# A vector of the adaptive layer norm moved from the sparse attention to the third FFN

## What is computed

```python
c_act = jax.nn.silu(c)
for i in range(DEPTH):                                   # DEPTH = 2
    mod = c_act @ ada_w[i] + ada_b[i]                    # 1024 -> 9 * 1024
    sh1, sc1, gt1, sh2, sc2, gt2, sh3, sc3, gt3 = jnp.split(mod, N_MOD, axis=-1)
    h = h + 0.5 * gt1 * swiglu(modulate(h, sh1, sc1), ffn_w_gu[i, 0], ffn_w_down[i, 0])
    u = modulate(h, sh2, sc2)
    m = dsa_mixer(u, ...) if i % 2 == 0 else rwkv7_mixer(u, ...)
    h = h + gt2 * m
    h = h + 0.5 * gt3 * swiglu(modulate(h, sh3, sc3), ffn_w_gu[i, 1], ffn_w_down[i, 1])
```

## Time and profile before

| | us |
|---|---|
| median of 3 runs | 1331.88 (1331.15 to 1332.82) |
| the profiled execution, in all | 1335.42 |
| its span in the profile | 1333.7 |
| TensorE busy | 1195.2 (90%), mean granted clock 0.911 |
| VectorE busy | 947.3 (71%) |
| ScalarE busy | 551.1 (41%) |
| the 256 multiply-adds of L1720 | 168.4 + 24.0 |

### The profile page before, as it was taken

The page is one execution under the profiler, slowest core; times in us unless marked ns, Lnnn a source line. Parts: engine busy times, 40 slices in busy tenths (PEclk is TensorE's granted clock), DMA queues, the critical chain, the costliest instruction groups (busy, mean ns, idle before and its releaser), DMA issues.

```text
span 1333.7 us, 20285 instructions
## 1 busy us (share of the span) xinstructions
PE 1195.2 (90%) x7950; PEld 943.0 (71%) x7950; DVE 947.3 (71%) x1291; ACT 551.1 (41%) x789; POOL 9.6 (1%) x27
## 2 busy tenths in 40 slices
PE   5799999877598899999899999798897968999998
PEld 1588887756256678887678888566676856788886
DVE  5888886876644788887788886698785495644443
ACT  2544444534233444444544444447341232444331
POOL 1000000000000000000000000000000000000000
PEclk9999999889557989999999999888896688999999
DMA  9789986563002678888578888421623020755540
GB/s 330 254 300 315 314 301 212 172 234 100 1 0 64 217 268 299 297 297 285 167 254 304 299 307 234 149 59 69 198 77 98 4 98 1 252 189 189 185 162 32
DMA packets 185852, 252.88 MB, mean 190 GB/s; under 512 B 30449, under 2 KB 121585, under 8 KB 185777
## 3 DMA queue, kind: packets, MB, share of 16 engines
q1 hardware_dynamic: 181554, 251.32, 56.2%
q10 hardware_dynamic: 4224, 0.52, 0.3%
HBM read 249.71 MB, written 2.10 MB: 189 GB/s over the span
## 4 chain that ended last, share of the span: by engine, by line
PE 75%; DVE 14%; DMA 4%; issue 3%; ACT 3%; SPq 1%; POOL 0%; DVEq 0%; ACTq 0%; POOLq 0%
PE bank L695 20%; PE bank L697 20%; PE bank L696 20%; DVE ada_acc L1720 2%; DVE gu_lo L1792 2%; PE bank L894 2%; DMA front<-in_ada_w_dram 1%; PE bank L755 1%; PE bank L1135 1%; PE bank L904 1%; PE bank L921 1%; PE bank L1020 1%; DVE dn_lo L1802 1%; ACT gu_hi L1269 1%; SPq L530 1%
## 5 line engine op out<-in xcount | busy, mean ns | idle before, releaser
L695 PE MATMUL bank<-gu_hi,xT_hi 128*128 128x512 f32 (+1 forms) x944 | 377.8, 400 | 34.0 <-DVE gu_lo L1792 9.1
L696 PE MATMUL bank<-gu_lo,xT_hi 128*128 128x512 f32 (+1 forms) x944 | 374.1, 396 | 0.0
L697 PE MATMUL bank<-gu_hi,xT_lo 128*128 128x512 f32 (+1 forms) x944 | 374.1, 396 | 0.0
L1792 DVE TENSOR_TENSOR gu_lo<-raw,gu_hi 128x2048 fp32r<-128x2048 f32 (+1 forms) x108 | 239.3, 2252 | 11.8 <-ACT gu_hi L1269 11.7
L695 PEld LDWEIGHTS bank<-gu_hi,xT_hi 128*128 128x128 f32 x944 | 182.6, 193 | 78.5 <-issue 16.0
L696 PEld LDWEIGHTS bank<-gu_lo,xT_hi 128*128 128x128 f32 x944 | 182.4, 193 | 39.1 <-issue 0.7
L697 PEld LDWEIGHTS bank<-gu_hi,xT_lo 128*128 128x128 f32 x944 | 181.9, 193 | 38.3
L1269 ACT CAST gu_hi<-raw 128x2048 fp32r<-128x2048 f32 (+1 forms) x108 | 199.7, 1881 | 18.4 <-DMA raw<-in_dsa_w_in_dram 8.0
L1720 DVE SCALAR_TENSOR_TENSOR ada_acc<-ada_raw,cact,ada_acc 128x512 f32<-128x512 f32 x224 | 168.4, 752 | 12.3 <-DMA ada_raw<-in_ada_w_dram 1.3
L695 PE MATMUL bank<-dn_hi,hT_hi 128*128 128x512 f32 x320 | 136.6, 427 | 6.6 <-DVE dn_lo L1802 6.6
L1802 DVE TENSOR_TENSOR dn_lo<-raw,dn_hi 128x2048 fp32r<-128x2048 f32 x40 | 91.7, 2291 | 68.2 <-ACT dn_hi L1280 68.2
(11 more groups left out here) (283 smaller groups left out, 1245.2 us busy)
## 6 DMA issues: line engine op xcount, KB each, us to landing
raw<-in_ffn_w_gu_dram SPq DMA_DIRECT2D x176, 512.0 KB, 8.9
ada_raw<-in_ada_w_dram SPq DMA_DIRECT2D x128, 512.0 KB, 6.7
raw<-in_ffn_w_down_dram SPq DMA_DIRECT2D x40, 1024.0 KB, 5.1
raw<-in_rwkv_w_rkv_dram SPq DMA_DIRECT2D x24, 512.0 KB, 5.0
raw<-in_dsa_w_in_dram SPq DMA_DIRECT2D x16, 512.0 KB, 5.1
front<-in_ada_w_dram SPq DMA_DIRECT2D x8, 512.0 KB, 7.8
last_raw<-in_ffn_w_down_dram SPq DMA_DIRECT2D x4, 1024.0 KB, 6.1
raw<-in_dsa_w_out_dram SPq DMA_DIRECT2D x8, 512.0 KB, 5.7
```

Source lines behind the costliest of these rows:

```text
L695: nc.tensor.matmul(out_ap, sta_hi, mov_hi, start=start, stop=False, skip_group_check=True)
L696: nc.tensor.matmul(out_ap, sta_hi, mov_lo, start=False, stop=False, skip_group_check=True)
L697: return nc.tensor.matmul(out_ap, sta_lo, mov_hi, start=False, stop=stop, skip_group_check=True)
L1792: nc.vector.tensor_tensor(gu_lo[:, par, ks, 0:width], buf[:, i, 0:4 * width].rearrange("p (k c) -> p k c", k=4), gu_hi[:, par, ks, 0:width ...
```

## The change

The attention builds two vectors, 14 and 15. Vector 16 is built in the first block of FFN 1, which has 16 to 25 now, and FFN 2 has 26 to 35, ten instead of nine. The waits on `mods_ready` follow the new numbers. `slice_of`, which maps a vector to its layer and column, is unchanged: in FFN 1 the first two belong to layer 0. With ten vectors, FFN 2 takes the branches that FFN 0 and FFN 1 take for the total of the tenth (`if nv == NB - 1`).

```diff
-    ADA_FFN = ((4, 10), (17, 10), (27, 9), (36, 0))
+    ADA_FFN = ((4, 10), (16, 10), (26, 10), (36, 0))
     ADA_DSA = 14
@@ sync, dsa
-                    if i in (1, 2, 3):
+                    if i in (1, 2):
                         load_ada(ADA_DSA - 1 + i, 0, ADA_DSA - 1 + i)
@@ tensor, dsa
-                    if i in (1, 2, 3):
+                    if i in (1, 2):
                         ada_total(ADA_DSA - 1 + i, TB[i % 2])
...
-                        pe.wait_ge(mods_ready, ADA_DSA + 3)
+                        pe.wait_ge(mods_ready, ADA_DSA + 2)
@@ vector, ffn
-                dve.wait_ge(mods_ready, (14, 27, 36, 36)[f])
+                dve.wait_ge(mods_ready, (14, 26, 36, 36)[f])
@@ vector, dsa
                 for i in range(3):
                     rest_in(i + 1)
-                    ada_products(ADA_DSA + i)
+                    if i < 2:
+                        ada_products(ADA_DSA + i)
```

## The result

The changed kernel took 1339.39 us in the median of 5 runs (1338.1 to 1344.95), the kernel before 1331.88 (1330.22 to 1335.25): a ratio of 1.006, 95% interval 1.0033 to 1.0086. Slower, and by more than forecast: +7.5 us where I had +4.0. (The ratios in this document are not the quotients of the medians beside them; the two can differ by 0.1%.)

The account below looks back on a forecast made before the run. TensorE carries three quarters of the chain, but its waits in the attention's projection and at the third FFN's end count. 10.4 - 6.4 = +4.0 us on the median 1331.88 gives 1335.9, range 1331.9 to 1339.6.

Parts of the forecast that it names:

- Attention, which wait goes: Attention's input projection: without vector 16's products the norm starts 7.3 us earlier, block 14 at 284.0, stall 1.1 us, not 8.4.
- What is late next: Attention: block 15 waits for its load, the q norm and the z copy; starts at 297.1 after a 2.1 us stall.
- Clock: Attention: block 14 stays at full clock; after the stall before block 15 the clock falls, a loss of 1.7 us.
- Attention, the size: Attention: block 15 begins 8.1 us earlier, less 1.7 us of clock, gain 6.4 us; bounds 2.6 to 8.8.
- Second FFN, nil: Second FFN: still builds ten vectors, 16 to 25, with equally large transfers covered by TensorE work; cost nil.
- Third FFN: Third FFN's end: later last down block delays RWKV's first weights' cast 10.1 us; with 0.3 of clock, cost 10.4 us.
- The sum: Whole kernel: third FFN's 10.4 less attention's 6.4 gives +4.0 us; 1339.4 on the profiled execution, 1335.9 as forecast median.
- The first (small loads not held): Third FFN's end: small loads are not held, delay 6.2 + 0.3, sum +0.1, 1332.0 us; chance 0.14.
- the second (the clock stays up): Attention's block 15: clock stays up as after the 1.56 us stall, sum +2.3, 1334.2 us; chance 0.12.
- the third (the attention keeps only 2.6 us): Attention: block 15's load lands late, gain 2.6, sum +7.8, 1339.7 us; chance 0.11.
- The fourth (the late cast is covered): Third FFN's end: k weights' cast waits without holding the silu; with cover for all -6.4, 1325.5 us; chance 0.07.

Follow-up runs that it names:

- this part alone: Kernel before with only the third FFN changed: it builds ten vectors, the last one made a second time as the tenth; 1344.14 us, ratio 1.0076.
- the silu's place: Changed kernel, at the third FFN's end the silu and hidden casts of the last block's first half come before rounding RWKV's first weights; 1335.95 us, ratio 1.0.
- before with small loads early: Kernel before with the ten small loads of the RWKV vectors issued at the end of SyncE's attention list; 1330.49 us, ratio 0.997.
- the changed kernel with both: Changed kernel with the ten small RWKV loads early and the silu before the next stage's weights in the first three FFNs; 1324.36 us, ratio 0.993.

## Why the prediction was right, and where it was wrong

- **Attention, which wait goes.** Right: block 14 starts at 283.55 (forecast 284.0), after a stall of 1.04 us (1.1).
- **What is late next.** Right in kind: block 15's load, the q norm, the z copy. The size was off: the second half of the load came 0.7 us later than I took it (287.70, not 287.0), block 15 started at 297.85 (297.1), and since block 14 ran at full clock the stall was 3.12 us (2.1; 2.72 and 2.75 in the other two traces).
- **Clock.** Right: behind the 3.12 us stall the granted clock (third from the end of each row, stretches of 1 us of the changed kernel) was 0.50, the lower of the two levels, until about 301.4, a loss of 0.02 + 3 x 0.50 + 0.19 = 1.7 us (1.7 forecast). The Trainium skill's rule that the prediction weighs at this step (TensorE: Matmul & The Clock Gate, "HAM oscillation — how this bites in real kernels") lays lost clock at long idle gaps; by it the clock would have stayed up here, and the trace disagrees.

```profile
297.00:298.00 1.00, 0.15 (x1) 0.16 (x2) 0.67 (x3) 0.91 (x3) 0.00 (x0) 0.98 0.03 10
298.00:299.00 1.00, 1.00 (x3) 0.81 (x4) 1.00 (x2) 1.00 (x2) 0.00 (x0) 0.50 0.00 0
...
301.00:302.00 1.00, 1.00 (x5) 0.81 (x4) 1.00 (x1) 0.88 (x1) 0.00 (x0) 0.81 0.00 0
```

- **Attention, the size.** The whole stage came out 6.2 to 6.4 us shorter in three traces; forecast 6.4. That it fits so well is partly luck. The projection, for which the 6.4 was worked out, gave 5.4 to 5.5 us (from the stage's start to its end 83.0 us before, 77.7 and twice 77.5 after); the other 0.9 us came behind it, where I had expected no change, and I didn't follow it. The late landing made 0.7 of the shortfall. Some of the rest lies in the start of block 15 before, which I put at 305.25, the end of the vector's sum; the trace has its first product at 304.68.
- **Second FFN, nil.** Right: 218.2 in two traces against 218.4; 219.5 in the first.
- **Third FFN.** The second FFN was the right template: 12.88 us (12.98), landing of the last block 5.1 us (5.0):

```profile
last_raw<-in_ffn_w_down_dram SPq DMA_DIRECT2D x1, 1024.0 KB, 5.1
```

  The fit of the Trainium skill that the prediction sets beside its row (DMA: Bandwidth & Descriptors, "Anatomy of one DMA — SWDGE (gpsimd) path") is given there for DMAs issued from GpSimd, while SyncE issues this one; its 4.4 us stands against 5.1 us measured. The third small load was again held, until 827.20 with the block landing at 827.46. Then the seven others took 4.9 us instead of 6.0, so the weights were issued 9.7 us after the last block (10.4), and their cast came 6.6 us later (6.1). Delay 9.7 us (10.1). The stage grew by 8.3 us in the first trace, 10.0 and 9.8 in the next two and 10.4 with this part alone; forecast 10.4. That "the queue is full" remains a reading: the traces show the hold and the landing, not the reason.
- **The sum.** By the stages, and against the first trace of before, attention, second and third FFN give +3.2, +3.5 and +3.3 us in the three traces of the changed kernel; forecast +4.0. By the ratios two of three comparisons say +2.8 and +3.2 us, the first +8.0; by the medians +5.0, +3.3 and +7.5.
- **The step that failed** is the last one: that the sum on the profiled execution may be moved down to the median of three runs. I took that execution (1335.42) as 3.5 us too slow and wrote 1335.9. It was an ordinary one: later medians of the same kernel are 1333.3 to 1335.2, and 1335.42 + 4.0 = 1339.4, the figure that the prediction had on the way, is near the changed kernel's three medians (1338.25 to 1339.39). That it meets the first of them to 0.1 us is luck. The change of +7.5 against +4.0 has the same root: the five runs of before in the first comparison were 1.4 to 3.4 us below its later medians, and the five of the changed kernel about 1 us above theirs. That this is chance in small samples, and nothing about that first round, is the likely reading and not shown. No term of the sum was off by 4 us.
- **Which rival came nearest.** None happened. The first (small loads not held) is refuted by the 3.29 us hold, the second (the clock stays up) by the 0.50 above, the third (the attention keeps only 2.6 us) by the 6.2. The fourth (the late cast is covered) is true of another program, as the silu's place shows.

## What to carry to other kernels

A wait on a DMA queue is paid by everything that is issued behind it, so before work is put in front of such a wait, read what stands behind: here ten loads of 4 KB that nobody needed yet made about 4 of the 10 us that the tenth vector cost, and moving them was worth 4.0 us to the kernel before and 7.9 to the changed one. Work that an engine does for the next stage (rounding its first weights) belongs behind what the current stage waits for, wherever its load can come late. Where the load is early it gained nothing: in the third FFN of before, small loads already early, the stage took 201.1 us with the silu first and 200.5 without. And a sum made on a profiled execution is to be compared with that execution; a median of three or five runs whose spread is as large as the effect is no better base.

## What the runs showed of the hardware

A load of 4 KB gathered element by element mostly costs SyncE 0.5 to 0.8 us to issue, but the third of them behind a 1 MB block was held until the block had nearly landed: 3.53 us in the first trace of before, 3.29 and 3.21 in two of the changed kernel, with the landing 0.5 us behind the hold's end in the first of these and 0.3 in the second. Behind two large blocks, in the kernel before, the second small load took 2.34 us as well.

The RWKV stage, of many small matmuls and short waits, took 265.5 to 273.2 us with the same instructions. Its mean granted clock was lowest in the longest and highest in the shortest, though not in step between them: 0.85 stood beside both 265.7 and 269.1 us. The stretches, with the clock third from the end of each row, from before (268.9 us), the changed kernel with the silu first (273.2), before with small loads early (265.5) and the changed kernel with both (265.7):

```profile
847.00:1116.00 269.00, 224.57 (x3852) 184.57 (x3850) 198.70 (x280) 104.05 (x203) 2.04 (x2) 0.84 0.27 82
```

```profile
846.00:1119.00 273.00, 224.07 (x3822) 184.56 (x3822) 198.30 (x280) 104.18 (x203) 2.04 (x2) 0.81 0.28 84
```

```profile
843.50:1109.00 265.50, 220.35 (x3851) 181.35 (x3849) 198.40 (x280) 104.19 (x203) 2.04 (x2) 0.86 0.28 84
```

```profile
836.00:1102.00 266.00, 222.23 (x3843) 181.97 (x3841) 198.72 (x281) 104.13 (x203) 2.03 (x2) 0.85 0.28 87
```

Between the clock of 0.81 and that of 0.86 lie 7.7 us, more than the effect of the change. Why one execution gets the one and one the other wasn't tried.
